# State copies of a decoder step: issued by GpSimd in the prompt attention stages instead of by ScalarE in the feed-forward stages

## What is computed

```python
def last_rows(a, n): return a[:, a.shape[1] - n:]          # cut to the case at hand
kv_b = jnp.concatenate([state_kv, jnp.stack([kb, vb], 2)], 1)
return ..., kv_b[:, -B_BUF:]     # mixer B: 8 x 2048 rows of 1024 float32; mixer C: 8 x 512 rows of 256 float32
```

## Time and profile before

| | us |
|---|---|
| median of 3 runs (lowest, highest) | 3461.7 (3436.59, 3471.76) |
| span of the profiled execution | 3459.9 |
| TensorE busy in the profiled execution | 2655.9 |

### The profile page before, as it was taken

One profiled execution on the slowest core, in us unless ns is written; L12 is line 12 of the kernel. 1 busy time (PEld: TensorE's weight loads), 2 busy tenths in 40 slices (PEclk: granted clock), 3 DMA queues, 4 the chain that ended last, 5 costly groups with the idle time before them and its releaser, 6 DMA issues. The chain is left out here.

```text
span 3459.9 us, 38384 instructions
## 1 busy us (share of the span) xinstructions
PE 2655.9 (77%) x13798; PEld 2027.6 (59%) x13802; DVE 1477.0 (43%) x2970; ACT 885.0 (26%) x1465; POOL 177.5 (5%) x404
## 2 busy tenths in 40 slices
PE   5976788686987777667967889977777777667596
PEld 2973333253556777666867745544555567667585
DVE  2223577555455333342342234654344433343334
ACT  1111111111232332233221122432323222333232
POOL 0000000000000111110000000000000011111000
PEclk9997788787588888879978556988889778888898
DMA  3352544222111433342123121133212123334321
GB/s 88 129 192 71 203 149 153 88 98 75 42 35 55 147 132 130 132 152 93 44 94 98 32 75 37 41 79 119 98 67 110 61 60 130 137 131 144 132 82 46
DMA packets 208838, 344.26 MB, mean 100 GB/s; under 512 B 32982, under 2 KB 144646, under 8 KB 204786
## 3 DMA queue, kind: packets, MB, share of 16 engines
q1 hardware_dynamic: 194992, 204.40, 19.5%
q10 hardware_dynamic: 10268, 83.75, 5.9%
q0 software_dynamic: 3456, 54.53, 4.1%
HBM read 315.74 MB, written 97.35 MB: 119 GB/s over the span
## 5 line engine op out<-in xcount | busy, mean ns | idle before, releaser
L216 PE MATMUL ffn_acc<-x_h,ffn_wh 128*128 128x288 f32 x1408 | 313.6, 306 | 217.5 <-DVE ffn_wl L208 217.5
L216 PEld LDWEIGHTS ffn_acc<-x_h,ffn_wh 128*128 128x128 f32 x1408 | 236.7, 197 | 220.0 <-issue 220.0
L208 DVE TENSOR_TENSOR ffn_wl<-ffn_w,ffn_wh 128x2048 fp32r<-128x2048 f32 (+1 forms) x88 | 154.4, 1754 | 410.8 <-ACT ffn_wh L1753 345.8
L216 PE MATMUL ffn_acc<-x_l,ffn_wh 128*128 128x288 f32 x1408 | 310.2, 303 | 0.0
L216 PE MATMUL ffn_acc<-x_h,ffn_wl 128*128 128x288 f32 x1408 | 309.5, 303 | 0.0
L216 PEld LDWEIGHTS ffn_acc<-x_l,ffn_wh 128*128 128x128 f32 x1408 | 236.0, 196 | 0.0
L216 PEld LDWEIGHTS ffn_acc<-x_h,ffn_wl 128*128 128x128 f32 x1408 | 235.2, 196 | 0.0
L1725 PE MATMUL ffn_acc<-ffn_wh,x_h 128*128 128x512 f32 x440 | 177.3, 403 | 69.2 <-DVE ffn_wl L208 69.2
L1726 PE MATMUL ffn_acc<-ffn_wl,x_h 128*128 128x512 f32 x440 | 174.6, 397 | 0.0
L1727 PE MATMUL ffn_acc<-ffn_wh,x_l 128*128 128x512 f32 x440 | 174.2, 396 | 0.0
L1753 ACT CAST ffn_wh<-ffn_w 128x2048 fp32r<-128x2048 f32 x44 | 84.0, 1910 | 316.8 <-DMA ffn_w<-ffn_up 316.8
(11 more groups left out here) (404 smaller groups left out, 5123.5 us busy)
## 6 DMA issues: line engine op xcount, KB each, us to landing
out_s_b_kv<-state_b_kv ACTq DMA_DIRECT2D x22, 2960.0 KB
ffn_w<-ffn_up SPq DMA_DIRECT2D x88, 512.0 KB, 5.7
ffn_w<-ffn_down SPq DMA_DIRECT2D x44, 512.0 KB, 3.7
sb_k<-state_b_kv SPq DMA_DIRECT2D x8, 2048.0 KB, 13.2
sb_v<-state_b_kv SPq DMA_DIRECT2D x8, 2048.0 KB
proj_ab_w<-w_in_ab SPq DMA_DIRECT2D x11, 1024.0 KB, 5.4
pc_table<-vec_up SPq DMA_DIRECT2D x8, 1280.0 KB, 8.3
proj_c_w<-w_in_c SPq DMA_DIRECT2D x7, 1024.0 KB, 5.4
```

What stands on the lines that cost most here:

```text
L208: return dve.tensor_tensor(low, whole, high.bitcast(F32), ALU.subtract)
L216: done = pe.matmul(o, weights, x, start=start, stop=stop)
```

## The change

The state copy leaves the feed-forward phases and goes into the prompt attention phases, layer 0's half into `pab` and layer 1's into `pc`. GpSimd issues it. A step is now two DMAs, each for 255 consecutive rows of one sequence, which are contiguous in HBM (1,044,480 bytes) on both sides. Steps 0 to 15 go with heads 0 to 15: step 0 at the start of the phase, step `n` when the scores of head `n-1` are done. Behind step 15 come four DMAs of 504 x 1024 bytes for mixer C's state. The wait for the copies stays at the end of the feed-forward phases, on ScalarE.

```diff
+class StateCopy:
+    ROWS = (PAST - NS) // 8
+    HEADS = 16
+    COUNT = 16 * (2 * HEADS + NB // 2)
...
+    def step(self, e, n):
+        for j in (2 * n, 2 * n + 1):
+            b, r = self.first + j // 8, j % 8 * self.ROWS
+            e.dma_start(self.dst_b[b, r:r + self.ROWS, :], self.src_b[b, NS + r:NS + r + self.ROWS, :]).then_inc(self.copied, 16)
+    def rest(self, e):
+        for b in range(self.first, self.first + NB // 2):
+            e.dma_start(self.dst_c[b, 0:C_WIN - NS, :], self.src_c[b, NS:C_WIN, :]).then_inc(self.copied, 16)
...
+        @block.gpsimd
+        def _(pool):
+            for n in range(len(heads)):
+                if n:
+                    pool.wait_ge(logit_ready, per_head * n)
+                state_copy.step(pool, n)
+            state_copy.rest(pool)
...
-    ROWS = (PAST - NS) // (NF // 2)
-    def step(self, e, i):
-        e.dma_start(self.dst_b[self.b, bass.ds(i * self.ROWS, self.ROWS), :],
-                    self.src_b[self.b, bass.ds(i * self.ROWS + NS, self.ROWS), :]).then_inc(self.copied, 16)
...
             def step(i, ahead):
-                state_copy.step(act, i)
...
-            state_copy.rest(act)
...
-            state_copy.wait(act)
+            act.wait_ge(copied, copied_count)
```

More of the change, by code:

```diff
@@ L484, in _, with __init__, prompt_attention_phase @@
                 dve.tensor_tensor(s, s, keep.causal[:, :], ALU.add).then_inc(summed, 1)
-def prompt_attention_phase(nc, name, branches, heads, hT, vec_up, tok, keep, tok_loads=(), sel_bias=None):
+class StateCopy:
+    ROWS = (PAST - NS) // 8
+    HEADS = 16
+    COUNT = 16 * (2 * HEADS + NB // 2)
+    def __init__(self, io, half, copied):
+        self.src_b, self.dst_b, self.src_c, self.dst_c = io["state_b_kv"], io["o_s_b_kv"], io["state_c_kv"], io["o_s_c_win"]
+        self.first, self.copied = half * NB // 2, copied
+    def step(self, e, n):
[5 more added lines that the diff above has]
+            e.dma_start(self.dst_c[b, 0:C_WIN - NS, :], self.src_c[b, NS:C_WIN, :]).then_inc(self.copied, 16)
+def prompt_attention_phase(nc, name, branches, heads, hT, vec_up, tok, keep, state_copy, tok_loads=(), sel_bias=None):
     with phase(nc, name) as p:
@@ L1543, in _, with ffn_phase @@
                 norm.low_part(dve, t, tps)
-class StateCopy:
-    ROWS = (PAST - NS) // (NF // 2)
-    def __init__(self, io, half, copied):
-        self.src_b, self.dst_b, self.src_c, self.dst_c = io["state_b_kv"], io["o_s_b_kv"], io["state_c_kv"], io["o_s_c_win"]
-        self.b, self.copied, self.before = slice(half * NB // 2, (half + 1) * NB // 2), copied, half * 16 * (NF // 2 + 2)
-    def step(self, e, i):
-        e.dma_start(self.dst_b[self.b, bass.ds(i * self.ROWS, self.ROWS), :],
-                    self.src_b[self.b, bass.ds(i * self.ROWS + NS, self.ROWS), :]).then_inc(self.copied, 16)
[L1561 to L1572, removed]
+def ffn_phase(nc, name, w_up, conv_w, conv_b, w_down, prev, g, b, p_tail, s_tail, y, copied, copied_count, keep):
     EXT = 2 + SEQ + NB * (2 + NS)
@@ L2610, in build @@
                 ], [(B_Q + h * HD, H_A + h, [(0, h)]) for h in range(H_B)] + [(A_Q + h * HD, h, [(1, h)]) for h in range(H_A)],
-                    dram.hT_ab, dram.vec_up, v_tok, keep, tok_loads=[
+                    dram.hT_ab, dram.vec_up, v_tok, keep, StateCopy(io, 0, copied), tok_loads=[
                     (v_tok[:, :, 0:P], io["o_p_a_kv"].rearrange("(i p) c -> p i c", p=P)[:, :, P:2 * P]),
@@ L2617, in build @@
             ffn_phase(nc, "ffn0", io["ffn_up"][0], io["ffn_conv_w"][0], io["ffn_conv_b"][0], io["ffn_down"][0], io["state_ffn"][0],
-                      io["ln2_g"][0], io["ln2_b"][0], io["o_p_ffn"][0], io["o_s_ffn"][0], None, StateCopy(io, 0, copied), keep)
+                      io["ln2_g"][0], io["ln2_b"][0], io["o_p_ffn"][0], io["o_s_ffn"][0], None, copied, StateCopy.COUNT, keep)
             project_phase(nc, "proj_c", io["w_in_c"], C_COLS, dram.hT_c, keep)
@@ L2634, in build @@
                 dict(heads=N_HEADS, k=C_KV + 4 * P, kv=2, v=5 * P, kind=KIND_WIN, h0=0, sel=False, gate=2 * N_HEADS),
-            ], [(C_Q + h * HD, h, [(0, h), (1, h)]) for h in range(N_HEADS)], dram.hT_c, dram.vec_up, tok, keep)
+            ], [(C_Q + h * HD, h, [(0, h), (1, h)]) for h in range(N_HEADS)], dram.hT_c, dram.vec_up, tok, keep, StateCopy(io, 1, copied))
         sample_c_phase(nc, dram.hT_c, dram.vec, io["cache_c_kv"], io["state_c_kv"], io["o_s_c_kv"],
@@ L2641, in build @@
                       io["ln2_g"][1], io["ln2_b"][1], io["o_p_ffn"][1], io["o_s_ffn"][1], (io["o_y_prompt"], io["o_y_sample"]),
-                      StateCopy(io, 1, copied), keep)
+                      copied, 2 * StateCopy.COUNT, keep)
 def t5_buckets(dist):
```

## The result

The changed kernel takes **3178.5 us** (median of 4 runs, 3154.4 to 3202.4) against 3463.4 us before (4 runs on the same chip): a ratio of **0.916, 95% interval 0.910 to 0.923**. The ratio and its interval leave out the changed kernel's longest run, which is over 1.5% above its fastest. The forecast was 3189 us, in a range of 3155 to 3260. The two later sets of six runs of the same kernel gave 3157.5 us each.

What follows compares the result with a forecast made beforehand. TensorE, busy 77% of the span, bounds the kernel and stalls on weights behind the four-engine state copy. 3459.9 - 289.5 gained + 17 cost = 3187 us, plus 1.8 for the runs' median: 3189 us, range 3155 to 3260.

Steps and rivals of the forecast that it cites:

- Up part: First part of `ffn0` and `ffn1`: without waits and restarts it should take about 283 us in place of 400.
- 211.4 us of waits: Up parts: TensorE's waits for the weights' low part, 108.2 and 109.2 us less 3.0 each, go completely.
- 23 us of restarts: Up parts: ten restarts after waits, at a granted clock of 0.52, cost 2.3 us each and go.
- the first wait: Down part's start: 15.15 and 14.12 us shrink to 9.3 us after the up part, gaining 10.6 us.
- the second wait: Down part: waits of 19.09 and 20.82 us go, with a restart of 2.3 us each, gaining 44.5 us.
- The rate of copying: HBM to HBM copies on 16 engines in the attention phases: 300 GB/s taken, between 208 and 430.
- The starts: Starts of `pab` and `pc`: step 0 collides with SyncE's first loads, 7 us each of the 17 us cost.
- the slower rival: Attention phases: GpSimd's queue uses few engines or sends pieces one after another; 3634 us with three engines; chance 0.03.
- 10.6 us for a head of `pab`: Attention phase `pab`: a head takes about 10.6 us, set against 4.9 to 10.0 us for its two pieces.
- four engines as the root: Feed-forward phases: the state copy, 4 sequences outermost, keeps four engines never idle at 107 GB/s; weight packets wait behind its packets.
- copying scales: Attention phases; the rival says 16 engines copy little faster than four: 3256 us at 160 GB/s, 3420 at 107; chance 0.09.
- the clock stayed at 0.99 over 283 us: Feed-forward phases; the rival says the clock falls to 0.86 in longer full-rate stretches, some 40 us a phase, 3270; chance 0.04.

## Why the prediction was right

**Up part.** Forecast 211.4 us of waits and 23 us of restarts, measured 116.9 + 116.1 = 233.0. The part should take about 283 us and took 283.2 and 285.1. (The 45 KB for a state packet was a mean over 72 records, four of which have 4 bytes; the packets of data have 47,360.)

**Down part.** Forecast 9.3 us for the first wait, and it is 9.3. With the second wait and its restarts the forecast was 55.1 us; the feed-forward stages without their up parts became 27.0 us shorter each, 54.0. The sum of the gains was put at 289.5 and came to 287.0.

**Cost.** The rate of copying was taken as 300 GB/s between 208 and 430; it is 384 while one piece flows, and 316 over the 37 us in which all copies had been sent at once (11.69 MB, beside some loads). The 214 GB/s that the Trainium skill gives for the best of the HBM to HBM copies in its table ("DMA: Bandwidth & Descriptors", section on latency and other measured facts) is not a ceiling for these pieces: they are contiguous, 65,280 bytes a packet, and measured 384. The starts cost 4.7 and 3.4 us where 7 each were put, and 2.0 us came at the end of `pab`: 10 us in place of 17. The same page of the Trainium skill says in its section on why a DMA increments its semaphore by 16 that a contiguous run can be split over all 16 engines, where an outermost dimension of 4 has 4. This was borne out, by 16 packets for a piece in one case and by four packets under way at a time with the old shape in the other. That GpSimd's successive pieces would lie on different engines when they use four was not foreseen; the slower rival thought of fixed ones.

**What the forecast left out.** It took 10.6 us for a head of `pab` as a fixed pace. That was a mean over heads of 13.4 us at the lower clock and 8.1 us at the upper. The profiled execution of before had 166 us for its heads, at the short end of what this stage does; the changed kernel's profile had 184.5. That hid 18 us in the comparison of spans. In the comparison of medians it is scatter, and there the forecast was 11 us too high against the first set and 31 against the later two, which lie 2.5 us above the lower end of the range. With a scatter of 25 us and more, hitting the first set within 11 is in part luck; what bears the prediction out is the sum by stage.

**What it gave the wrong weight.** The argument named four engines as the root, but costed only the move. The old place with the new shape brings the same time (3173.7 and 3178.5 us), and the new place with the old shape nearly the same (3202.0 us), with no stall either. So move and shape were not two gains but two ways to the same one, and the shape alone would have done. What the shape adds to the move is the start of the attention stages, 27.6 us less delay. Of the rivals, none came: copying scales, the clock stayed at 0.99 over 283 us, and GpSimd's queue used all engines.

## What to carry to other kernels

When a small load waits for a large background copy, look first at how many DMA engines the copy uses: a steady 25% of 16 engines, beside a second queue that gets one small packet through for each large one, points to a copy whose outermost dimension is too small. Making its runs contiguous is a change of a few lines and can be all that's needed; moving it away from the loads helps too. A background copy must still be paced, since a burst of large packets delays every load of many small packets that meets it (here 35.5 MB a stage put off the first scores by 77 and 102 us).

## What the runs showed of the hardware

The float32 score and transpose matmuls of `pab` keep TensorE busy for 80 us of 80 and yet at a granted clock of 0.50; the stage goes over to 1.00 at a moment that differs between executions. There it stayed to the end of the heads in all profiles but one, where TensorE had waited 2.86 us, in `pab` and in `pc` alike, and went on at 0.50. Activity from before didn't carry over (52 spare matmuls, then 0.50 within 4 us of the first scores of `pab`), while one 128x512 bf16 matmul more in each step went with a clock of 1.00 from the first head of `pab` in both profiles that had it, and 136.8 us for the heads. It did not do so in `pc`, which had them in one profile and ran at 0.50 for the first 63 us.

An engine moved a 65,280-byte packet from HBM to HBM in 2.72 us with all 16 at work, 24 GB/s each, for 27 GB/s each with four at work. On ScalarE's queue a copy with an outermost dimension of 4 kept to four engines at a time over the whole 30 us; on GpSimd's queue successive ones overlapped, eight engines at a time.
